# The 256th score of every query: two 16-step searches on halves of the bits against one 32-step search shared by VectorE and ScalarE

## The chip, the core and the metric

The kernel runs on one core of a Trainium2 chip. The metric is the device time of one execution in microseconds (us), taken as the median of the runs. TensorE is written PE here, its weight loads PEld, VectorE is DVE, ScalarE is ACT, GpSimd is POOL, and SP is SyncE, which issues most of the DMA transfers. The profile gives the clock that was granted to TensorE as a share of 2.4 GHz: 1.00 is 2.4 GHz and 0.50 is 1.2 GHz.

## What is computed

The program is one inference step of a two-layer decoder, for a prompt of 1024 tokens and for 8 sequences of 4 new tokens with 2048 cached positions each. The change lies in the second layer, whose attention is sparse: an indexer gives every query a score against every earlier key, the 256 best keys are kept, and attention runs over those alone.

```python
def index_scores(qi, wi, ki):
    s = jnp.einsum('bthd,bsd->bths', qi, ki).astype(jnp.float32)
    return jnp.einsum('bths,bth->bts', jax.nn.relu(s), wi.astype(jnp.float32))

# for each block of 128 prompt queries
sc = index_scores(qib, wib, ki)
sc = jnp.where((key_pos[None, :] <= tq[:, None])[None], sc, -jnp.inf)
_, sel = lax.top_k(sc, n_sel)                     # n_sel = 256
valid = sel <= tq[None, :, None]
return sparse_attend(qb, k[b_idx, sel], v[b_idx, sel], valid)
```

The sample queries do the same over their 2048 cached keys and the new ones. `top_k` takes equal scores in the order of their position. The layer, like every one, is modulated by `silu(c) @ w + b`; the product for the last sublayer is computed in the same phase as the search.

## The kernel before

The phase of the program that matters is `index_phase`. It holds the scores of the prompt in `sc`, 128 partitions (one per query of a block) by 4224 columns of f32: six blocks of queries, whose rows are 384, 512, 640, 768, 896 and 1024 keys long (`SC0` gives where each begins). The first two blocks of the prompt have no more than 256 keys and need no search. The 32 sample queries lie in `scs`, 128 by 513, each query's keys spread over four partitions.

**The search.** The kernel keeps no sorted list. It finds each query's 256th score bit by bit: a candidate threshold is formed by setting one more bit (`c.bits` holds one constant per step), the scores that are not below it are counted, and the bit stays if the count is at least 256. There are seven thresholds per partition (`NC`), one for each of the six blocks and one for the sample queries, in `fbits`. In a step (`search_step`, L1161 to L1175) DVE forms the candidate `cand` (L1163), counts the sample scores (L1165), counts the six blocks (L1182), reads from PSUM the sample count that PE has summed over the four partitions (L1168), compares the counts with 256 (L1170) and updates `fbits` (L1172). The next step needs that result, so the steps stand in a row. A count is a `tensor_scalar` that compares, with `accum_out` summing the row:

```python
dve.tensor_scalar(junk[:, w], sch[:, w], cf[:, b:b + 1], 0.0, ALU.is_ge, ALU.add, accum_out=cnt[:, b:b + 1])
```

The search runs in two halves. The first 16 steps (L1184) count on `sch`, the upper 16 bits of the scores as bf16, copied beforehand (L1159). Then L1190 to L1203 count what lies above, mark the scores whose upper half equals the found one and cut out their lower 16 bits. The second 16 steps (L1213) count on those, with one conversion and one addition more per step (L1206, L1211). L1215 puts the two halves together. After that every block is counted once more on the f32 scores, ties are settled by position with a scan, and the mask for the attention is written (L1219 to L1254).

**What runs beside it.** PE has a queue in program order: `total(i)` (L1067), the sum of the sample counts for step i, stands between the pieces of the modulation product. For each of its 12 units of weights u (`MU`), the order is total(2u), `multiply(u)` (L179), total(2u+1), `turn(u)` (L192). A multiply is 8 matmuls of 256 columns in f32, which the profile shows as 16 passes. The weights of a unit, 1 MB, land in `vT`, which holds one unit: SP issues the load of unit u+1 (L975) when multiply(u) has finished with it (`used`).

```python
for i in range(2 * MU):
    total(i)
    if i % 2 == 0:
        if i:
            pe.wait_ge(row_ready, i // 2)
        mod.multiply(pe, i // 2)
    else:
        mod.turn(pe, i // 2)
```

ACT copies the sums of a unit out of PSUM (L186) and has nothing else to do during the search. Behind the weights SP issues 16 loads of the sample cache (L1440). When DVE is through with the masks, all engines meet and the attention of the prompt begins.

Of the kernel before, what the change touches and what calls it, by code (L numbers as in the profile page):

```python
# [40 lines left out]
MU = 3 * D // 256  # L41
# [859 lines left out]
def index_phase(nc, c, d):  # L901

    with ExitStack() as ctx:
        sb = lambda n, s, dt=F32: ctx.enter_context(nc.sbuf_tensor(f"ix_{n}", s, dt))
        sem = lambda n: c.new_sem(f"ix_{n}")
        sc = sb("sc", [P, SCW])
# [10 lines left out]
        fbits, cand, acc = sb("fbits", [P, NC], I32), sb("cand", [P, NC], I32), sb("acc", [P, NC], I32)  # L917
        cnt, part, need = sb("cnt", [P, NC]), sb("part", [P, 3]), sb("need", [P, NC + 1])
        tot = sb("tot", [P, 2, 3])
        thi, above, candf, keep = sb("thi", [P, NSEL]), sb("above", [P, NSEL]), sb("candf", [P, NSEL]), sb("keep", [P, NSEL], I32)  # L920
        mrow = rs[0:NSQ, :, 0:256]
        junk = sb("junk", [P, SCW], BF16)

# [2 lines left out]

        cum = rel[:, 0:2, :]
        words = rel[:].rearrange("p a n -> p (a n)").bitcast(BF16)
        sch, junks = words[:, 0:SCW], words[:, SCW:SCW + SKW + 1]
# [177 lines left out]
        @block.vector  # L1107
        def _(dve):
            k = [0]

            def link(ins):

                k[0] += 1
                ins.then_inc(step, 1)
                dve.wait_ge(step, k[0])
# [13 lines left out]
            n = 0  # L1129
# [21 lines left out]
            link(dve.tensor_tensor(scs[:, SKW:SKW + 1], c.ps[:, 7, 0:1], c.newkey[:, 0:1], ALU.add))  # L1151


            link(dve.tensor_copy(fbits[:], c.bits[:, 0:1].to_broadcast([P, NC])))
            dve.wait_ge(causal, NSEL)
            cf, ff = cand[:].bitcast(F32), fbits[:].bitcast(F32)
# [4 lines left out]
            def search_step(i, s0, prompt_counts, extra):  # L1161

                dve.tensor_tensor(cand[:], fbits[:], c.bits[:, bass.ds(i, 1)].to_broadcast([P, NC]), ALU.bitwise_xor).then_inc(sel, 1)  # L1163
                dve.wait_ge(sel, s0 + 1)
# [9 lines left out]
                dve.wait_ge(sel, s0 + (10 + extra))
                dve.wait_ge(part_ready, i + 1)  # L1175

            def blocks():
                return [(b, slice(SC0[q], SC0[q] + (q + 1) * P)) for b, q in enumerate(BLK)]

            def upper_counts(s1):  # L1180
                for b, w in blocks():
                    dve.tensor_scalar(junk[:, w], sch[:, w], cf[:, b:b + 1], 0.0, ALU.is_ge, ALU.add, accum_out=cnt[:, b:b + 1]).then_inc(sel, 1)  # L1182

            with dve.Fori(0, 16) as i:  # L1184
                search_step(i, i * 10, upper_counts, 0)

            link(dve.tensor_copy(thi[:], fbits[:, 0:NSEL].bitcast(BF16).rearrange("p (n two) -> p n two", two=2)[:, :, 1]))  # L1190
            for b, w in blocks():
                ins = dve.tensor_scalar(junk[:, w], sch[:, w], thi[:, b:b + 1], 0.0, ALU.is_gt, ALU.add, accum_out=above[:, b:b + 1])
            link(ins)
            for b, w in blocks():
                ins = dve.tensor_scalar(junk[:, w].bitcast(I16), sch[:, w], thi[:, b:b + 1], -1.0, ALU.is_equal, ALU.mult)
            link(ins)
            low = sc[:].bitcast(U16).rearrange("p (n two) -> p n two", two=2)[:, :, 0]
            for b, w in blocks():
                y = junk[:, w].bitcast(U16)
                ins = dve.scalar_tensor_tensor(out=y, in0=low[:, w], scalar=fbits[:, b:b + 1].bitcast(U16)[:, 0:1], in1=y,  # L1200
                                               op0=ALU.bitwise_xor, op1=ALU.bitwise_and)
            link(dve.tensor_copy(keep[:], fbits[:, 0:NSEL]))
            link(dve.tensor_tensor(fbits[:, 0:NSEL], keep[:], keep[:], ALU.bitwise_xor))  # L1203

            def lower_counts(s1):
                dve.tensor_copy(candf[:], cand[:, 0:NSEL]).then_inc(sel, 1)  # L1206
                dve.wait_ge(sel, s1 + 1)
                for b, w in blocks():
                    dve.tensor_scalar(sch[:, w], junk[:, w].bitcast(U16), candf[:, b:b + 1], 0.0, ALU.is_ge, ALU.add, accum_out=cnt[:, b:b + 1]).then_inc(sel, 1)
                dve.wait_ge(sel, s1 + 7)  # L1210
                dve.tensor_tensor(cnt[:, 0:NSEL], cnt[:, 0:NSEL], above[:], ALU.add).then_inc(sel, 1)  # L1211
# [541 lines left out]
def build(nc, d):  # L1753
    with ExitStack() as ctx:
# [19 lines left out]
        c.bits = sb("bits", [P, 32], I32)  # L1774
# [45 lines left out]
def tables():  # L1820
# [91 lines left out]
```

## Time and profile before

| | us |
|---|---|
| median of 3 runs (lowest to highest) | 3023.41 (3021.97 to 3024.28) |
| the profiled execution: its span, first to last instruction | 3025.1 |
| of it, DVE from the first instruction of the search (L1154) to the first behind it (L201) | 1350.13 to 1597.86 |
| the first 16 steps | 112.0 |
| between the two halves | 13.6 |
| the second 16 steps | 119.2 |

The profiled execution is 1.7 us above the median of the runs. The stretches of the table are read from the table of busy times by window. In such a table a row is a stretch in us from the start of the span; behind its length stands the busy time of each engine with the number of its instructions, and then the granted clock of PE, the busy share of the DMA engines and GB/s. In the timelines a row is the start in us, the duration in us, the engine, the line, the operation, what it writes and reads, and in brackets how long the engine was idle before it and whom it waited for. In the groups, the two numbers behind the bar are busy time in us and the mean duration of one instruction in ns. Instructions of one engine overlap a little: the distance between two starts is shorter than the duration of the first.

### The profile page before, as it was taken

To read this page: it belongs to the slowest core of one execution; us is meant where nothing else is said; L and a number is where in the kernel's file an instruction comes from. 1 tells how busy PE (TensorE), PEld (TensorE's weight loads), DVE (VectorE), ACT (ScalarE), POOL (GpSimd) and SP (SyncE) were. 2 spreads that over 40 slices of the span, in tenths; PEclk is the share of its full clock that TensorE was granted. 3 is DMA by queue.
4 is the path that set the end of the run, shared out by engine and by line. 5 is a ranking of instruction groups with operands and counts; after the bars stand their busy time and mean duration, and the time that the engine had idled before them with its cause. 6 is when DMAs were issued, how large, how long until landed. Compare 5 with 4: busy or idle time off the path is not lost. (4 is left out here: it accounts for less than half of the span.)

```text
span 3025.1 us, 40642 instructions
## 1 busy us (share of the span) xinstructions
PE 2520.1 (83%) x14573; PEld 2225.2 (74%) x14573; DVE 1439.8 (48%) x3100; ACT 694.4 (23%) x1162; POOL 744.9 (25%) x557
## 2 busy tenths in 40 slices
PE   7866999999999689784312789697869999999995
PEld 3446999999999589741112567345869999999994
DVE  2747333333333730179997578344273333333336
ACT  2113111111110322150001888312131111111101
POOL 0223121121121235410000677521131211221110
PEclk9887999999999799896655999888979999999997
DMA  9421111111110234552121110571011111111101
GB/s 368 166 94 56 42 42 42 42 42 69 42 42 14 99 113 162 152 121 81 56 69 28 39 32 16 182 268 56 29 56 42 42 42 42 42 64 47 42 14 57
DMA packets 89864, 230.67 MB, mean 76 GB/s; under 512 B 15764, under 2 KB 52724, under 8 KB 73396
## 3 DMA queue, kind: packets, MB, share of 16 engines
q1 hardware_dynamic: 75856, 205.33, 19.6%
q0 software_dynamic: 10400, 22.18, 2.3%
q10 hardware_dynamic: 3524, 2.07, 0.2%
q8 instruction: 49, 0.80, 0.1%
q14 instruction: 35, 0.29, 0.0%
HBM read 200.77 MB, written 28.76 MB: 76 GB/s over the span
## 5 line engine op out<-in xcount | busy, mean ns | idle before, releaser
L676 PE MATMUL ps<-f_hhi,f_whi 128*128 128x352 f32 x2112 | 687.2, 325 | 33.9 <-DVE f_hlo L348 18.4
L677 PE MATMUL ps<-f_hhi,f_wlo 128*128 128x352 f32 x2112 | 681.7, 323 | 0.0
L678 PE MATMUL ps<-f_hlo,f_whi 128*128 128x352 f32 x2112 | 680.9, 322 | 0.0
L647 POOL TENSOR_TENSOR f_wlo<-f_raw,f_whi 128x2048 fp32r<-128x2048 f32 x66 | 304.0, 4607 | 1110.1 <-ACT f_whi L623 1110.1
L80 DVE SCALAR_TENSOR_TENSOR xT<-ps,mod,xT 128x352 f32<-128x352 f32 (+1 forms) x576 | 327.9, 572 | 219.8 <-PE ps L698 121.4
L676 PEld LDWEIGHTS ps<-f_hhi,f_whi 128*128 128x128 f32 x2112 | 400.4, 190 | 37.6 <-DVE f_hlo L348 37.6
L677 PEld LDWEIGHTS ps<-f_hhi,f_wlo 128*128 128x128 f32 x2112 | 401.0, 190 | 0.0
L678 PEld LDWEIGHTS ps<-f_hlo,f_whi 128*128 128x128 f32 x2112 | 400.1, 189 | 0.0
L696 PE MATMUL ps<-f_ahi,f_whi 128*128 128x352 f32 x1056 | 340.6, 323 | 0.0
L697 PE MATMUL ps<-f_ahi,f_wlo 128*128 128x352 f32 x1056 | 338.3, 320 | 0.0
L698 PE MATMUL ps<-f_alo,f_whi 128*128 128x352 f32 x1056 | 338.1, 320 | 0.0
L623 ACT ACTIVATE f_whi<-f_raw 128x2048 fp32r<-128x2048 f32 x66 | 126.4, 1915 | 554.2 <-PE ps L698 418.2
L1396 POOL TENSOR_TENSOR pa_pr<-pa_pr,pa_rl 128x128 f32<-128x128 f32 (+7 forms) x128 | 142.8, 1147 | 368.1 <-DVE pa_rl L1376 368.0
L716 DVE TENSOR_TENSOR f1n_g<-f1n_sq,ps 128x352 f32<-128x352 f32 x66 | 34.4, 521 | 399.4 <-PE ps L678 396.9
L716 DVE TENSOR_TENSOR f0n_g<-f0n_sq,ps 128x352 f32<-128x352 f32 x66 | 34.4, 521 | 398.1 <-PE ps L678 395.7
L697 PEld LDWEIGHTS ps<-f_ahi,f_wlo 128*128 128x128 f32 x1056 | 198.4, 188 | 0.0
L696 PEld LDWEIGHTS ps<-f_ahi,f_whi 128*128 128x128 f32 x1056 | 198.1, 188 | 0.0
L698 PEld LDWEIGHTS ps<-f_alo,f_whi 128*128 128x128 f32 x1056 | 197.9, 187 | 0.0
L876 PE MATMUL ps<-pj_hhi,pj_whi 128*128 128x352 f32 x408 | 135.0, 331 | 19.0 <-DVE pj_hlo L354 11.0
L1067 PE MATMUL ps<-ix_part,rowsum 128*128 128x1 f32 x64 | 16.3, 324 | 156.3 <-DVE ix_rel L1165 156.2
L179 PE MATMUL ps<-ada_raw,silu 128*9 128x256 f32 x576 | 129.2, 388 | 14.5 <-ACT silu L431 14.5
L1316 PE MATMUL ps<-kst,pa_qst 128*128 128x512 f32 (+3 forms) x192 | 75.2, 392 | 73.7 <-DMA pa_qst<-halves 41.7
(307 smaller groups left out, 3939.0 us busy)
## 6 DMA issues: line engine op xcount, KB each, us to landing
f_raw<-in_ffn SPq DMA_DIRECT2D x66, 1024.0 KB, 4.8
ada_raw<-in_ada SPq DMA_DIRECT2D x36, 1024.0 KB, 5.0
sa_kv<-in_ckv POOLq DMA_DIRECT2D x54, 256.0 KB, 4.3
ix_vT<-in_ada SPq DMA_DIRECT2D x12, 1024.0 KB, 4.8
sa_kv<-in_ckv SPq DMA_DIRECT2D x42, 256.0 KB, 4.4
pj_raw<-in_win SPq DMA_DIRECT2D x9, 1024.0 KB, 5.8
pa_qst<-halves SPq DMA_DIRECT2D x128, 64.0 KB, 2.4
halves<-pj_shi SPq DMA_DIRECT2D x45, 176.0 KB, 1.9
```

The costliest lines, as they stand in the source:

```text
L80: ins = dve.scalar_tensor_tensor(out=x, in0=psum[:, 0:n], scalar=gate[:, 0:1], in1=x, op0=ALU.mult, op1=ALU.add)
L179: last = pe.matmul(self.sums(u), self.c.silu[:, k, :], w[:, k, :], start=(k == 0), stop=(k == KD - 1))
L623: act.activation(whi[:, a, :], raw[:, a % 2, :], ACT.Copy).then_inc(w_hi, 1)
L647: pool.tensor_tensor(wlo[:, a, :], raw[:, a % 2, :], whi[:, a, :].bitcast(F32), ALU.subtract).then_inc(w_lo, 1)
L676: pe.matmul(c.ps[:, bank, 0:CH], hi[:, k, side, :], hhi[:, k, col], start=(k == 0), stop=False)
L677: pe.matmul(c.ps[:, bank, 0:CH], lo[:, k, side, :], hhi[:, k, col], start=False, stop=False)
L678: last = pe.matmul(c.ps[:, bank, 0:CH], hi[:, k, side, :], hlo[:, k, col], start=False, stop=(k == KD - 1))
L696: pe.matmul(c.ps[:, q % 6, 0:CH], hi[:, k, w], ahi[:, k, col], start=(k == 0), stop=False)
L697: pe.matmul(c.ps[:, q % 6, 0:CH], lo[:, k, w], ahi[:, k, col], start=False, stop=False)
L698: last = pe.matmul(c.ps[:, q % 6, 0:CH], hi[:, k, w], alo[:, k, col], start=False, stop=(k == 1))
L876: pe.matmul(c.ps[:, q, 0:CH], hi[:, k, w], hhi[:, k, col], start=(k == 0), stop=False)
L1396: pool.tensor_tensor(p, p, rl[:, i % 3, g:g + 1].to_broadcast([P, (q + 1) * P]), ALU.mult).then_inc(p_ready, 1)
```

## The change

The two halves become one loop of 32 steps that counts on the f32 scores themselves. There is no upper half, no lower half and nothing between them. In each step DVE counts the sample scores and the three short blocks (384, 512 and 640 keys); ACT counts the three long blocks (768, 896 and 1024) with `Sign`: the sum of the signs of (candidate − score) over a row tells how many scores lie below. `signs(i)` waits for the candidate of step i (`cand_ready`), and DVE waits for the three sums (`signs_ready`) before it compares all counts with the limits in `lim`. The candidate for the next step is formed in one operation with the update of the last. A score that equals the candidate gives a sign of 0, so a threshold of the long blocks can end a step beside a tied score; this is settled once at the end (L1202 to L1214). PE's queue and SP's keep their order.

```diff
+            def signs(i):
+                act.wait_ge(cand_ready, i + 1)
+                for b, w in blocks(SGN):
+                    last = act.activation(junk[:, w], sc[:, w], ACT.Sign, bias=cand[:, b:b + 1].bitcast(F32), scale=-1.0,
+                                          accum_out=cnt[:, b:b + 1])
+                last.then_inc(signs_ready, 1)
+
             for u in range(MU):
+                signs(2 * u)
+                signs(2 * u + 1)
                 mod.copy_sums(act, u)
+            with act.Fori(2 * MU, 32) as i:
+                signs(i)
...
-            link(dve.tensor_copy(sch, sc[:].bitcast(BF16).rearrange("p (n two) -> p n two", two=2)[:, :, 1]))
...
+            with dve.Fori(0, 32) as i:
+                s0 = i * (SGN + 3)
                 dve.tensor_scalar(junks[:], scs[:], cf[:, NSEL:NC], 0.0, ALU.is_ge, ALU.add, accum_out=part[:, 0:1]).then_inc(part_ready, 1)
-                prompt_counts(s0 + 1)
+                for b, w in blocks(0, SGN):
+                    dve.tensor_scalar(junk[:, w], sc[:, w], cf[:, b:b + 1], 0.0, ALU.is_lt, ALU.add, accum_out=cnt[:, b:b + 1]).then_inc(sel, 1)
                 dve.wait_ge(tot_ready, i + 1)
+                dve.tensor_scalar(diff[:, NSEL:NC], c.ps[:, 4, 0:1], TOPK - 0.5, None, ALU.subtract).then_inc(sel, 1)
+                dve.wait_ge(signs_ready, i + 1)
+                dve.wait_ge(sel, s0 + SGN)
+                dve.tensor_tensor(diff[:, 0:NSEL], lim[:], cnt[:, 0:NSEL], ALU.subtract).then_inc(sel, 1)
...
+                dve.tensor_scalar(miss[:], diff[:].bitcast(I32), 31, c.bits[:, bass.ds(i, 1)], ALU.arith_shift_right, ALU.bitwise_and).then_inc(sel, 1)
...
+                dve.scalar_tensor_tensor(out=cand[:], in0=cand[:], scalar=c.bits[:, bass.ds(i + 1, 1)], in1=miss[:],
+                                         op0=ALU.bitwise_xor, op1=ALU.bitwise_xor).then_inc(cand_ready, 1)
+                dve.wait_ge(cand_ready, i + 2)
...
+            for b, w in blocks(SGN):
+                y = cum[:, b % 2, 0:w.stop - w.start]
+                dve.tensor_scalar(junk[:, w], sc[:, w], cf[:, b:b + 1], 0.0, ALU.is_gt, ALU.add, accum_out=cnt[:, b:b + 1])
+                link(dve.tensor_scalar(y, sc[:, w], cf[:, b:b + 1], -1.1 * NEG, ALU.is_le, ALU.mult))
+                link(dve.tensor_tensor_reduce(out=y, in0=y, in1=sc[:, w], scale=1.0, scalar=-NEG, op0=ALU.add, op1=ALU.min, accum_out=above[:, b:b + 1]))
```

On ACT, before, the copies of the modulation sums stand alone during the search, behind the last ReLU of the scores (`ix_rs` is the row buffer of the sums):

```order
L1103 ACTIVATE ix_rn<-ps 128x4
L186 ACTIVATE ix_rs<-ps 9x256 x12
```

and now six counts, those of two steps, stand ahead of each copy:

```order
L1115 ACTIVATE ix_junk,ix_cnt<-ix_sc,ix_cand 128x896
L1115 ACTIVATE ix_junk,ix_cnt<-ix_sc,ix_cand 128x1024
L186 ACTIVATE ix_rs<-ps 9x256
L1115 ACTIVATE ix_junk,ix_cnt<-ix_sc,ix_cand 128x768
L1115 ACTIVATE ix_junk,ix_cnt<-ix_sc,ix_cand 128x896
L1115 ACTIVATE ix_junk,ix_cnt<-ix_sc,ix_cand 128x1024
```

The copies kept their order among themselves; 96 counts moved onto the engine around them.

On DVE a step of the first loop was, before, from the candidate to the update (REGISTER_ALU rows work out the number that a wait compares with):

```order
L1163 TENSOR_TENSOR ix_cand<-ix_fbits,bits 128x7
L1164 ISA
L1165 TENSOR_SCALAR ix_rel,ix_part<-ix_rel,ix_cand 128x513
L1182 TENSOR_SCALAR ix_junk,ix_cnt<-ix_rel,ix_cand 128x384
L1182 TENSOR_SCALAR ix_junk,ix_cnt<-ix_rel,ix_cand 128x512
L1182 TENSOR_SCALAR ix_junk,ix_cnt<-ix_rel,ix_cand 128x640
L1182 TENSOR_SCALAR ix_junk,ix_cnt<-ix_rel,ix_cand 128x768
L1182 TENSOR_SCALAR ix_junk,ix_cnt<-ix_rel,ix_cand 128x896
L1182 TENSOR_SCALAR ix_junk,ix_cnt<-ix_rel,ix_cand 128x1024
L1167 REGISTER_ALU
L1168 TENSOR_SCALAR ix_acc<-ps 128x1
```

and now the step is, with three counts fewer and one wait more (the ISA row of L1189 waits for ACT):

```order
L1183 TENSOR_SCALAR ix_rel,ix_part<-ix_rel,ix_cand 128x513
L1185 TENSOR_SCALAR ix_junk,ix_cnt<-ix_sc,ix_cand 128x384
L1185 TENSOR_SCALAR ix_junk,ix_cnt<-ix_sc,ix_cand 128x512
L1185 TENSOR_SCALAR ix_junk,ix_cnt<-ix_sc,ix_cand 128x640
L1186 REGISTER_ALU
L1187 TENSOR_SCALAR ix_diff<-ps 128x1
L1189 ISA
L1190 TENSOR_TENSOR ix_diff<-ix_lim,ix_cnt 128x6
```

The sums of the sample scores still come first, and the read of PE's total still stands behind the counts.

PE's rows of this stretch are the same in both kernels; a unit of the modulation with the totals around it reads, in the changed kernel:

```order
L1073 MATMUL ps<-ix_part,rowsum 128x1
L179 MATMUL ps<-ix_vT,silu 9x256 x8
L1073 MATMUL ps<-ix_part,rowsum 128x1
L192 MATMUL ps<-ident,ix_rs 128x9 x2
L1073 MATMUL ps<-ix_part,rowsum 128x1
```

So the total of every odd step stands behind a multiply, as it did before.

## Rows read from the trace of the kernel before

**Rows 1.** The profile's first line.

```profile
span 3025.1 us, 40642 instructions
```

**Rows 2.** Busy times by window: first half, between, second half of the search.

```profile
1352.90:1464.90 112.00, 54.92 (x176) 22.62 (x176) 104.88 (x288) 2.99 (x8) 0.00 (x0) 0.69 0.21 75
1464.90:1478.50 13.60, 0.00 (x0) 0.00 (x0) 12.94 (x27) 0.00 (x0) 0.00 (x0) 0.50 0.00 1
1478.50:1597.70 119.20, 31.57 (x104) 15.19 (x104) 110.58 (x321) 1.49 (x4) 0.00 (x0) 0.60 0.19 62
```

**Rows 3.** DVE's timeline: the search's first row, its second step, the first row behind.

```profile
1350.13 0.17 DVE L1154 COPY ix_fbits<-bits 128x7 int32<-128x7 int32 x1
...
1360.17 0.75 DVE L1165 TENSOR_SCALAR_CACHE_REDUCE ix_rel<-ix_rel,ix_cand 128x513 bf16<-128x513 f32 x1
...
1360.84 0.61 DVE L1182 TENSOR_SCALAR_CACHE_REDUCE ix_junk<-ix_rel,ix_cand 128x384 bf16<-128x384 bf16 x1
...
1362.84 1.00 DVE L1182 TENSOR_SCALAR_CACHE_REDUCE ix_junk<-ix_rel,ix_cand 128x768 bf16<-128x768 bf16 x1
...
1366.04 0.15 DVE L1168 TENSOR_SCALAR ix_acc<-ps 128x1 int32<-128x1 f32 x1
1366.15 0.17 DVE L1170 TENSOR_SCALAR ix_acc<-ix_cnt 128x6 int32<-128x6 f32 x1
1366.36 0.23 DVE L1172 SCALAR_TENSOR_TENSOR ix_fbits<-ix_acc,bits,ix_fbits 128x7 int32<-128x7 int32 x1
1366.98 0.17 DVE L1163 TENSOR_TENSOR ix_cand<-ix_fbits,bits 128x7 int32<-128x7 int32 x1 [0.39 <-DVE ix_fbits L1172]
...
1597.86 0.38 DVE L201 TENSOR_TENSOR mod<-ps,vec 128x216 f32<-128x216 f32 x1
```

**Rows 4.** DVE's groups of 1024 columns: counts, a comparison, sums of two tensors.

```profile
L1182 DVE TENSOR_SCALAR_CACHE_REDUCE ix_junk<-ix_rel,ix_cand 128x1024 bf16<-128x1024 bf16 x16 | 20.4, 1275 | 0.0
L1363 DVE CUSTOM_DVE_ANT_0 pa_pr<-ps,mb 128x1024 f32<-128x1024 f32 x16 | 19.4, 1215 | 0.0
L1140 DVE SCALAR_TENSOR_TENSOR ix_sc<-ix_rel,wtok,ix_sc 128x1024 f32<-128x1024 f32 x7 | 9.0, 1284 | 0.8 <-ACT ix_rel L1093 0.2
L1248 DVE SCALAR_TENSOR_TENSOR ix_vT<-ix_rel,ix_need,ix_vT 128x1024 bf16<-128x1024 f32 x1 | 1.3, 1285 | 0.0
L1244 DVE TENSOR_SCALAR_CACHE_REDUCE ix_junk<-ix_sc,ix_fbits 128x1024 bf16<-128x1024 f32 x1 | 1.3, 1279 | 0.0
L1245 DVE TENSOR_SCALAR ix_vT<-ix_sc,ix_fbits 128x1024 bf16<-128x1024 f32 x1 | 0.8, 750 | 0.0
```

**Rows 5.** ACT's groups: the exponentials of the prompt's attention, which sum their rows.

```profile
L1425 ACT ACTIVATION_READ_ACCUMULATOR pa_pr<-pa_pr,pa_nb 128x1 f32 x128 | 24.2, 189 | 0.0
L1425 ACT ACTIVATE pa_pr<-pa_pr,pa_nb 128x1024 f32<-128x1024 f32 x16 | 18.4, 1148 | 0.2
L1425 ACT ACTIVATE pa_pr<-pa_pr,pa_nb 128x896 f32<-128x896 f32 x16 | 16.7, 1042 | 0.3
L1425 ACT ACTIVATE pa_pr<-pa_pr,pa_nb 128x768 f32<-128x768 f32 x16 | 15.0, 934 | 0.4
```

**Rows 6.** The loads of the modulation weights: issues, and time to landing.

```profile
L975 SPq DMA_DIRECT2D ix_vT<-in_ada x12: 328/328/592, 1331.8 to 1515.6; - x12
...
DMA to landing us min/median/max: 4.8/4.8/22.3
```

**Rows 7.** PE: the multiplies as a group, one burst, one total; then warm weight loads.

```profile
L179 PE MATMUL ps<-ix_vT,silu 128*9 128x256 f32 x192 | 68.3, 534 | 0.0
...
1368.51 6.41 PE L179 MATMUL ps<-ix_vT,silu 128*9 128x256 f32 x16
...
1375.01 0.38 PE L1067 MATMUL ps<-ix_part,rowsum 128*128 128x1 f32 x2
...
1357.27 1.60 PEld L179 LDWEIGHTS ps<-ix_vT,silu 128*9 128x9 f32 x8 [0.15 <-issue]
```

**Rows 8.** Busy times by window: inside a multiply, right after another, and later.

```profile
1368.60:1374.30 5.70, 5.70 (x14) 1.81 (x15) 5.24 (x15) 0.00 (x0) 0.00 (x0) 0.51 0.00 0
1430.30:1435.50 5.20, 0.60 (x4) 0.49 (x4) 5.20 (x13) 0.37 (x1) 0.00 (x0) 1.00 0.54 202
1435.70:1438.60 2.90, 0.47 (x2) 0.47 (x2) 2.44 (x11) 0.00 (x0) 0.00 (x0) 0.50 0.00 0
```

More of the change, by code:

```diff
@@ L916, in index_phase @@
         NC = NSEL + 1
-        fbits, cand, acc = sb("fbits", [P, NC], I32), sb("cand", [P, NC], I32), sb("acc", [P, NC], I32)
+        cand, miss = sb("cand", [P, NC], I32), sb("miss", [P, NC], I32)
+        lim, diff = sb("lim", [P, NSEL]), sb("diff", [P, NC])
         cnt, part, need = sb("cnt", [P, NC]), sb("part", [P, 3]), sb("need", [P, NC + 1])
         tot = sb("tot", [P, 2, 3])
-        thi, above, candf, keep = sb("thi", [P, NSEL]), sb("above", [P, NSEL]), sb("candf", [P, NSEL]), sb("keep", [P, NSEL], I32)
+        tie, above = sb("tie", [P, 2, NSEL]), sb("above", [P, NSEL])
         mrow = rs[0:NSQ, :, 0:256]
@@ L928, in index_phase @@
         words = rel[:].rearrange("p a n -> p (a n)").bitcast(BF16)
-        sch, junks = words[:, 0:SCW], words[:, SCW:SCW + SKW + 1]
+        junks = words[:, SCW:SCW + SKW + 1]
         eq = vT[:, 0, :].bitcast(BF16)[:, 0:2 * SEQ].rearrange("p (a n) -> p a n", a=2)
@@ L937, in index_phase @@
         step, sel, tot_ready, ws_ready = sem("step"), sem("sel"), sem("tot_ready"), sem("ws_ready")
+        cand_ready, signs_ready = sem("cand_ready"), sem("signs_ready")
         part_ready, ki_out, ada_ready = sem("part_ready"), sem("ki_out"), sem("ada_ready")
@@ L941, in index_phase, with blocks @@
         BLK = list(range(SEL0, QT))
+        SGN = 3
+        def blocks(first=0, last=NSEL):
+            return [(b, slice(SC0[BLK[b]], SC0[BLK[b]] + (BLK[b] + 1) * P)) for b in range(first, last)]
         mod = Modulation(c, mrow, lambda u: vT[:].rearrange("p a n -> p (a n)")[:, 0:UNIT], lambda pe, u: pe.wait_ge(ada_ready, 16 * (u + 1)),
@@ L1151, in _ @@
             link(dve.tensor_tensor(scs[:, SKW:SKW + 1], c.ps[:, 7, 0:1], c.newkey[:, 0:1], ALU.add))
-            link(dve.tensor_copy(fbits[:], c.bits[:, 0:1].to_broadcast([P, NC])))
+            for b, w in blocks():
+                dve.memset(lim[:, b:b + 1], float(w.stop - w.start - TOPK) + (0.5 if b < SGN else TOPK - 510.5))
             dve.wait_ge(causal, NSEL)
-            cf, ff = cand[:].bitcast(F32), fbits[:].bitcast(F32)
-            link(dve.tensor_copy(sch, sc[:].bitcast(BF16).rearrange("p (n two) -> p n two", two=2)[:, :, 1]))
@@ L1174, in search_step @@
[L1174 to L1185, printed above, removed]
@@ L1190, in _ @@
[L1190 to L1196, printed above, removed]
@@ L1197, in _ @@
[L1197 to L1211, printed above, removed]
@@ L1213, in _ @@
-            with dve.Fori(16, 32) as i:
-                search_step(i, i * 12 - 32, lower_counts, 2)
-            link(dve.tensor_tensor(fbits[:, 0:NSEL], fbits[:, 0:NSEL], keep[:], ALU.bitwise_xor))
+                dve.tensor_scalar(diff[:, NSEL:NC], c.ps[:, 4, 0:1], TOPK - 0.5, None, ALU.subtract).then_inc(sel, 1)
+                dve.wait_ge(signs_ready, i + 1)
+                dve.wait_ge(sel, s0 + SGN)
+                dve.tensor_tensor(diff[:, 0:NSEL], lim[:], cnt[:, 0:NSEL], ALU.subtract).then_inc(sel, 1)
@@ new lines, in _ @@
+                dve.wait_ge(sel, s0 + (SGN + 2))
+                dve.tensor_scalar(miss[:], diff[:].bitcast(I32), 31, c.bits[:, bass.ds(i, 1)], ALU.arith_shift_right, ALU.bitwise_and).then_inc(sel, 1)
+                dve.wait_ge(sel, s0 + (SGN + 3))
+                dve.scalar_tensor_tensor(out=cand[:], in0=cand[:], scalar=c.bits[:, bass.ds(i + 1, 1)], in1=miss[:],
+                                         op0=ALU.bitwise_xor, op1=ALU.bitwise_xor).then_inc(cand_ready, 1)
+                dve.wait_ge(cand_ready, i + 2)
@@ new lines, in _ @@
+            ff = cf
+            sg = slice(SGN, NSEL)
+            link(dve.tensor_scalar(tie[:, 1, sg], cf[:, sg], 2.0 ** -126, None, ALU.is_ge))
+            link(dve.scalar_tensor_tensor(out=tie[:, 0, sg], in0=cf[:, sg], scalar=-2.0 ** -126, in1=tie[:, 1, sg], op0=ALU.is_le, op1=ALU.max))
+            link(dve.tensor_tensor(cf[:, sg], cf[:, sg], tie[:, 0, sg], ALU.mult))
+            for b, w in blocks(SGN):
[3 more added lines that the diff above has]
+                link(dve.tensor_tensor_reduce(out=y, in0=y, in1=sc[:, w], scale=1.0, scalar=-NEG, op0=ALU.add, op1=ALU.min, accum_out=above[:, b:b + 1]))
@@ L1217, in _ @@
+            link(dve.tensor_scalar(tie[:, 0, sg], cnt[:, sg], TOPK - 0.5, None, ALU.is_ge))
+            dve.tensor_tensor(above[:, sg], above[:, sg], tie[:, 0, sg], ALU.mult)
+            link(dve.tensor_scalar(tie[:, 1, sg], tie[:, 0, sg], 1.0, -NEG, ALU.subtract, ALU.mult))
+            link(dve.tensor_tensor(above[:, sg], above[:, sg], tie[:, 1, sg], ALU.add))
+            link(dve.tensor_tensor(cf[:, sg], cf[:, sg], above[:, sg], ALU.max))
             mod.apply(dve, SUBS - 1, MU, 0, link)
@@ L1773, in build @@
         c.invc = sb("invc", [P, 4, 16])
-        c.bits = sb("bits", [P, 32], I32)
+        c.bits = sb("bits", [P, 33], I32)
         c.rowsum, c.before = sb("rowsum", [P, P]), sb("before", [P, P])
@@ L1829, in tables @@
     t["invc"] = inv
-    bits = [-1] + [1 << (30 - i) for i in range(31)]
+    bits = [-1] + [1 << (30 - i) for i in range(31)] + [0]
     t["bits"] = np.tile(np.array(bits, np.int32), (P, 1))
```

12 lines of the change are left out of this document (3 added, 9 removed).

## The prediction

> **What bounds the kernel now.** The span is 3025.1 us [rows 1], 1.7 us above the median of the runs, so a saving in the profile is taken off the median as it stands. I read first the busy times by window of the search [rows 2]: DVE works in 104.88 of 112.00 us of the first half, 12.94 of 13.60 us between the halves and 110.58 of 119.20 us of the second, while ACT works for 4.5 us in all and PE for 86. DVE's timeline [rows 3] then shows why: a step is one string of instructions, the only gap is 0.39 us at the turn of the loop, and each step needs the result of the last. From the first row to the first behind the search it is 1597.86 − 1350.13 = 247.7 us. All engines meet behind it, so a us less here is a us less in the end.
>
> **What a step costs now and then.** Before, it is 112.00/16 = 7.0 us and 119.20/16 = 7.45 us [rows 2]. Its parts [rows 3]: sample count 0.67 (1360.17 to 1360.84), three short blocks 2.00 (to 1362.84), three long blocks 3.20 (to 1366.04), then the comparisons and update.
>
> The change counts on f32 instead of 16-bit words. That costs DVE nothing: the 1024-column count takes 1275 ns on bf16 and 1279 ns on f32 [rows 4]. So DVE's work ahead of its waits is the turn of the loop, 0.40, and 0.67 + 2.00 + 0.08 for the last sum: 3.15 us after the candidate. The first comparison (0.12 to the next start) ends at 3.27.
>
> ACT's part has no row of its own. The nearest is the exponential, which also takes a bias per partition and sums its row: 934, 1042 and 1148 ns for the three lengths, and 189 ns to read a sum [rows 5]. Back to back the read hides behind the next instruction except the last: 0.93 + 1.04 + 1.15 − 0.10 + 0.19 = 3.21 us. With 0.05 us of signalling at each end it is 3.3 us after the candidate. From below it is bounded by DVE's own 3.27, since ACT's rows all rise by 0.84 ns a column and none is faster; from above I keep 3.8, half a us for signalling and for a sign slower than the exponential. The two engines end level, at 3.3. Then come three small operations in a row; by the distances of L1170 and L1172 (0.21) and the 0.23 of the last [rows 3], 0.65. **A step by itself is 3.3 + 0.65 + 0.1 of slack for the new waits = 4.05 us**, range 3.9 to 4.6. Queued behind DVE's new wait for ACT are only these three operations; behind ACT's wait for the candidate stands one copy of sums for every six counts, 2.99/8 = 0.37 us [rows 2], which fits into the 0.65 us when ACT has nothing to do.
>
> **Where 4.05 us does not decide.** PE's queue keeps its order, and that is the term I weigh most. The total of an odd step stands behind a multiply. The multiplies form a chain of their own: a burst ends, SP issues the next MB, it lands 4.8 us later [rows 6], the next burst runs. A burst takes 68.3/12 = 5.69 us on average and 6.41 in the row shown [rows 7]. Two steps before took 14 us, which hid 4.9 (with 0.1 for signalling) + 5.69 = 10.6 us entirely; two steps of 4.05 take 8.1 us and do not. So in the first 24 steps a pair of steps costs one load and one burst.
>
> What a burst takes depends on the clock. Inside the 6.41 us burst the granted clock is 0.51, 1.2 GHz, for its first 14 passes, 0.41 us apiece; at 2.4 GHz eight weight loads stand in 1.60 us, 0.20 apiece [rows 7, 8]. The clock goes up during a burst and has come down before the next: after one burst it was still 1.00 in 1430.3 to 1435.5, and 0.50 from 1435.7 [rows 8]. Bursts now follow one another after 4.9 us instead of 14.0 − 5.69 = 8.3, so some will begin before the clock has fallen. I take 5.3 us, somewhat under the mean of 5.69, and **10.2 us for a pair**. Bounds: sixteen passes at 0.20 give 3.3, a pair of 8.2, which is no longer than two steps; sixteen at 0.41 give 6.6, a pair of 11.5.
>
> The Trainium skill ("TensorE: Matmul & The Clock Gate", section "HAM oscillation — how this bites in real kernels") says that a burst of matmuls shorter than the DMA wait after it starts at the low clock every time. By that rule no burst would begin at 2.4 GHz, and the pair would be the rows' mean or more. The trace agrees in part: it shows the low clock at the start of a burst (0.51), but after gaps of 8.3 us.
>
> **The sum.** The first weights are issued at 1331.8 and land after 22.3 us, at 1354.1 [rows 6]; DVE is ready earlier (the bf16 copy ahead of the loop falls away, seven small fills come instead), so multiply 0 starts at 1354.1 in any case and hides the setup. Eleven pairs: 112.2. The last burst: 5.3. Its total, the comparisons and the update, 0.4 + 0.05 + 0.12 + 0.65 = 1.2. Step 24 starts at 1354.1 + 112.2 + 5.3 + 1.2 = 1472.8. Eight steps alone: 32.4, to 1505.2.
>
> Then the ties, new: per long block a count, a comparison and a reduction of two tensors; at 1024 columns 1279 + 750 + 1215 ns [rows 4], the last from the nearest row, which reads PSUM. The three blocks are 2688 columns, 2.625 times that, 8.5 us; nine small operations at some 0.2 us and the reads of sums bring it to **11 us**, range 9.5 to 13. The search ends at 1516.2 in place of 1597.86: **81.7 us less**. The rest of the span, mask, attention and the second FFN, is untouched; the 16 cache loads move ahead with the end of the weights and have the last steps and the masks to land. Forecast: 3025.1 − 81.7 = 2943.4 us in the profile, **2942 us** as a median.
>
> **The rivals.** *Cold bursts*: every burst runs at 1.2 GHz throughout, 6.6 us, because PE's gaps let the clock fall each time. Eleven pairs longer by 1.3 and one burst: 11 × 1.3 + 1.3 = 16 us more, 2958. For it speaks the burst of 6.41; against it that the mean is 5.69. *Warm bursts*: the shorter gap keeps 2.4 GHz. A pair then costs 8.2, 11 × 2.0 + 2.0 = 24 us less, 2918; two steps of 4.05 set the same floor. The clock's 5.2 us of grace [rows 8] speaks for it, the 0.51 inside the burst of 1368.60 against it. *No overlap*: ACT and DVE both read `sc`, and would slow each other until a step is the sum of both parts, 3.15 + 3.3 + 0.65 = 7.1 us: 32 × 7.1 + 11 = 238 of the 247.7 us, 10 less, 3014; the change would then not do what it says. Against it: the DVE sum of 1024 columns takes 1284 ns with ACT writing beside it and 1285 ns with ACT idle [rows 4]. *Slow signs*, the one that ends slower than before: if a sign summed on ACT takes over twice the exponential's time, the counts last 6.7 us, a step 7.4, and 32 × 7.4 + 11 = 248 us is what the search takes today; at two and a half times, 8.0 us, a step is 8.7 and the search 289 us, 42 more, so 3066. The trace shows ACT at 1148 ns against DVE's 1275 for 1024 columns, so this needs an effect that no row has.
>
> The Trainium skill ("ScalarE: Activation LUTs", section "Rules for kernel authors") advises VectorE over ScalarE for simple elementwise work, up to about three times faster per element in bf16; that speaks against this change. With its factor of three the signs would last 3 × 3.2 = 9.6 us, a step 10.4 and the kernel, as an estimate, 3120. The trace disagrees for counts: on DVE they gain nothing from bf16 (1275 against 1279 ns), and ACT's rows are the shorter ones.
>
> **How the numbers follow.** Forecast 0.68 (with its own bounds, pairs of 9.7 to 10.8, steps and ties: 2933 to 2953), cold bursts 0.14, warm bursts 0.14, no overlap 0.02, slow signs 0.02. The range must take in the forecast and one side beside it: from 2930, part of the way to warm bursts, to 2960, which holds cold bursts: 0.68 + 0.14 and a little. Faster by over 0.2% (6 us, about what a measurement of this kernel can tell from no change): 0.97; slower 0.02; within 0.01.
>
> **What would show it.** In the profile after, the groups of signs should read about 0.93, 1.04 and 1.15 us; the first 24 steps should start in pairs some 10.2 us apart, with DVE idle in every odd step behind PE's total and not behind ACT; the last eight steps should stand 4.05 us apart with both engines done within 0.2 us; the clock should be near 0.5 at the start of most bursts. Wrong would be pairs of 8.2 us with DVE waiting for ACT (the loads do not bind), signs longer than the exponentials, or a search that shrank while the span did not.

## The result, and the profile after

| | before | after |
|---|---|---|
| median (lowest to highest) | 3023.85 us (3021.97 to 3029.91), 4 runs | 2943.67 us (2942.05 to 2944.72), 4 runs |
| ratio, 95% interval | | 0.9727 [0.9714, 0.9739] |
| profiled span | 3025.1 | 2942.1 |
| from the first sample count to the first instruction behind the search | 1353.13 to 1597.86 | 1349.28 to 1516.46 |
| from there to the end of the span | 1427.2 | 1425.6 |

The forecast was 2942.0, the range 2930 to 2960. The gain lies in the search: it ends 81.4 us earlier, and behind it the kernel takes what it took, but for 1.6 us. Of the 81.4 us, 1.2 had come about before the search: DVE's copy of the sample scores ahead of it (L1150, now L1169) starts at 1348.11 us in after and at 1349.35 in before, and that is scatter, for in the changed kernel once more (e8, below) it starts at 1350.02. Lines have moved by a few; L1183 is now the sample count (L1165), L1185 a DVE count (L1182), L1115 a sign on ACT, L1190, L1192 and L1194 the comparison and the update, L1073 the total (L1067), L981 the load (L975). Where [rows 1] stood, the page of after has:

```profile
span 2942.1 us, 40633 instructions
```

The window of the first 24 steps answers to [rows 2] (same columns: length, busy PE, PEld, DVE, ACT, POOL, clock, DMA share, GB/s):

```profile
1348.90:1472.40 123.50, 74.60 (x264) 30.30 (x264) 83.27 (x295) 81.21 (x157) 0.00 (x0) 0.83 0.32 111
```

DVE was busy 94% of the first half of the old search; in the first 24 steps it is now busy 83.27 of 123.50 us, 67%, and ACT 81.21. No engine is full in this window, so the time must lie in a chain that passes from engine to engine. The waits of the search (who waited for whom: total us, times, longest) name it:

```profile
PE ps L179 <- DMA ix_vT<-in_ada: 25.3, 12, 2.3
DVE ix_diff L1187 <- PE ps L1073: 22.6, 12, 2.1
DVE ix_rel L1183 <- DVE ix_cand L1194: 11.8, 31, 0.4
DVE ix_diff L1190 <- ACT ix_junk L1115: 0.3, 1, 0.3
```

DVE waits 12 times for PE's total, about 1.9 us each, in the odd steps only, and PE waits 12 times for weights. PE's timeline shows the period (its rows answer to [rows 7]):

```profile
1352.52 5.31 PE L179 MATMUL ps<-ix_vT,silu 128*9 128x256 f32 x16 [2.05 <-DMA ix_vT<-in_ada]
1357.76 0.38 PE L1073 MATMUL ps<-ix_part,rowsum 128*128 128x1 f32 x2
...
1362.81 5.30 PE L179 MATMUL ps<-ix_vT,silu 128*9 128x256 f32 x16 [2.05 <-DMA ix_vT<-in_ada]
...
1465.51 5.21 PE L179 MATMUL ps<-ix_vT,silu 128*9 128x256 f32 x16 [2.13 <-DMA ix_vT<-in_ada]
```

The total of the odd step stands right behind the burst. From the first burst to the twelfth it is 1465.51 − 1352.52 = 113.0 us, 10.27 a pair of steps: a burst of 5.2 us and 5.0 us from its end to the start of the next. The loads still land in 4.8 us as in [rows 6]; the longest, 22.1 us, is the first:

```profile
L981 SPq DMA_DIRECT2D ix_vT<-in_ada x12: 327/328/592, 1330.4 to 1460.5; - x12
...
DMA to landing us min/median/max: 4.8/4.8/22.1
```

The same wait from DVE's side, in its timeline; then the last candidate and the first row behind the search:

```profile
1349.28 0.75 DVE L1183 TENSOR_SCALAR_CACHE_REDUCE ix_rel<-ix_rel,ix_cand 128x513 bf16<-128x513 f32 x1 [0.23 <-DVE ix_cand L1176]
...
1358.17 0.16 DVE L1187 TENSOR_SCALAR ix_diff<-ps 128x1 f32<-128x1 f32 x1 [1.72 <-PE ps L1073]
1358.28 0.17 DVE L1190 TENSOR_TENSOR ix_diff<-ix_lim,ix_cnt 128x6 f32<-128x6 f32 x1
...
1505.74 0.23 DVE L1194 SCALAR_TENSOR_TENSOR ix_cand<-ix_cand,bits,ix_miss 128x7 int32<-128x7 int32 x1
...
1516.46 0.38 DVE L201 TENSOR_TENSOR mod<-ps,vec 128x216 f32<-128x216 f32 x1
```

The last eight steps have no burst in them and stand 4.24 us apart. One of them, in the timeline of all engines, from a candidate to the next:

```profile
1476.08 0.23 DVE L1194 SCALAR_TENSOR_TENSOR ix_cand<-ix_cand,bits,ix_miss 128x7 int32<-128x7 int32 x1
1476.34 0.93 ACT L1115 ACTIVATE ix_junk<-ix_sc,ix_cand 128x768 bf16<-128x768 f32 x1 [1.05 <-DVE ix_cand L1194]
1476.68 0.75 DVE L1183 TENSOR_SCALAR_CACHE_REDUCE ix_rel<-ix_rel,ix_cand 128x513 bf16<-128x513 f32 x1 [0.38 <-DVE ix_cand L1194]
...
1479.33 0.18 ACT L1115 ACTIVATION_READ_ACCUMULATOR ix_junk<-ix_sc,ix_cand 128x1 f32 x1
...
1479.35 0.15 DVE L1187 TENSOR_SCALAR ix_diff<-ps 128x1 f32<-128x1 f32 x1
1479.65 0.17 DVE L1190 TENSOR_TENSOR ix_diff<-ix_lim,ix_cnt 128x6 f32<-128x6 f32 x1
1479.95 0.23 DVE L1192 TENSOR_SCALAR ix_miss<-ix_diff,bits 128x7 int32<-128x7 int32 x1
1480.31 0.23 DVE L1194 SCALAR_TENSOR_TENSOR ix_cand<-ix_cand,bits,ix_miss 128x7 int32<-128x7 int32 x1
```

Both engines are through at 1479.5, within 0.1 us of each other. ACT is the later one by a little. Its path adds up to the step: 0.26 to its first sign, 3.17 to the end of its last sum, 0.14 to the comparison, then 0.30 and 0.36 to the next candidate, 4.23 in all. DVE's own path does not: 0.60 to the sample count, 2.67 to L1187, 0.11 to the comparison (the distance at 1358.17, where ACT had long been done; it is 0.11 in the last steps of e3 too, where ACT has less to do), 0.30 and 0.36 give 4.04. So ACT sets the step, by 0.19 us.

The groups of signs, which answer to the exponentials of [rows 5] (busy us, mean ns):

```profile
L1115 ACT ACTIVATE ix_junk<-ix_sc,ix_cand 128x1024 bf16<-128x1024 f32 x32 | 36.2, 1133 | 0.0
L1115 ACT ACTIVATE ix_junk<-ix_sc,ix_cand 128x896 bf16<-128x896 f32 x32 | 32.8, 1026 | 0.0
L1115 ACT ACTIVATE ix_junk<-ix_sc,ix_cand 128x768 bf16<-128x768 f32 x32 | 29.9, 935 | 33.5 <-DVE ix_cand L1194 31.7 <-DVE ix_cand L1176 1.8
L1115 ACT ACTIVATION_READ_ACCUMULATOR ix_junk<-ix_sc,ix_cand 128x1 f32 x96 | 17.9, 186 | 0.0
```

A sign takes what an exponential takes, with DVE reading the same scores beside it. DVE is not slowed either: its counts of 384 keys take 608 ns on average here, in before and in e4, where ACT counts nothing. The clock inside one burst (start 1404.1), by window, answers to [rows 8]:

```profile
1404.10:1404.50 0.40, 0.40 (x2) 0.11 (x3) 0.27 (x2) 0.00 (x0) 0.00 (x0) 0.50 0.00 0
1404.60:1407.50 2.90, 2.90 (x9) 0.93 (x8) 2.52 (x8) 2.86 (x5) 0.00 (x0) 0.53 0.02 6
1407.90:1409.20 1.30, 1.30 (x7) 0.39 (x5) 0.00 (x0) 0.00 (x0) 0.00 (x0) 1.00 0.00 0
1413.00:1414.00 1.00, 0.00 (x0) 0.00 (x0) 0.86 (x4) 0.86 (x2) 0.00 (x0) 1.00 0.40 164
```

The burst starts at 1.2 GHz and ends at 2.4. The clock then stays at 2.4 GHz to within 0.3 us of the next burst (start 1414.28), although PE does nothing in 1413.0 to 1414.0, and that burst reads 0.50 again in its first 0.4 us. Of the twelve bursts ten read 0.50 in their first 0.4 us, the other two 0.72 and 0.64. The Trainium skill ("TensorE: Matmul & The Clock Gate", section "HAM oscillation — how this bites in real kernels") describes a kernel whose bursts are shorter than the wait for their data, and start at the low clock every time. The trace agrees with it on ten of twelve starts, though a burst here, at 5.2 us, is not shorter than the 5.0 us between two of them.

### The profile page after: what moved, and what is told of

Read it like the earlier page. It is cut to its first block and busy times, and to the rows that moved or that the text cites. A ratio compares the mean times of both kernels' runs of the same rounds, so it can differ in the third digit from the quotient of the medians.

```text
span 2942.1 us, 40633 instructions
## 1 busy us (share of the span) xinstructions
PE 2510.8 (85%) x14573; PEld 2220.6 (75%) x14573; DVE 1328.1 (45%) x2876; ACT 796.7 (27%) x1354; POOL 743.8 (25%) x557
## 5 line engine op out<-in xcount | busy, mean ns | idle before, releaser
L877 PE MATMUL ps<-pj_hhi,pj_wlo 128*128 128x352 f32 x408 | 133.8, 328 | 0.0
```

What stands on the lines that cost most here:

```text
L877: pe.matmul(c.ps[:, q, 0:CH], lo[:, k, w], hhi[:, k, col], start=False, stop=False)
```

## The experiments

Three theories stood. *Loads and bursts*: in the first 24 steps a pair of steps costs one load and one burst, whatever a step costs; the last eight cost a step each. *The step*: what DVE and ACT do in a step, and the small operations behind it, sets the time throughout. *Contention*: one engine slows the other. Every edit below is made on the changed kernel. The median of before on these chips was 3027.24 us for the first four (12 runs) and 3025.77 for the last four (7 runs). Beside the median I give the search, from the first sample count to L201, 167.2 us in after, since the rest of the span scatters: from 1416.9 (e6) and 1418.6 (e3) to 1427.7 us (e4), with nothing changed in it. A difference in the medians of less than 10 us is therefore read from the search.

**e1: a second buffer for the weights.** Units land by turns in `vT` and in `rel`, which is idle during the search, so a load no longer waits for the burst before it.

```diff
+        wbuf = [t[:].rearrange("p a n -> p (a n)")[:, 0:UNIT] for t in (vT, rel)]
...
-                if u:
-                    sp.wait_ge(mod.used, u)
+                if u > 1:
+                    sp.wait_ge(mod.used, u - 1)
+                elif u:
+                    sp.wait_ge(r_used, NIH * NSEL)
...
-                sp.dma_start(vT[:].rearrange("p a n -> p (a n)")[:, 0:UNIT], d.ada[(SUBS - 1) * MU + u]).then_inc(ada_ready, 16)
+                sp.dma_start(wbuf[u % 2], d.ada[(SUBS - 1) * MU + u]).then_inc(ada_ready[u % 2], 16)
```

> The changed kernel with a second buffer for the modulation weights (in the score buffer that the search no longer uses), so that unit u+1 is loaded while unit u is multiplied. Theory (in the first 24 steps a pair of steps is bound by one load of 4.8 us and one burst of 5.2 us in a row, 10.27 us): without the load in the row a pair is two steps of 4.24 us, 8.5 us; 11 pairs shorter by 1.8 and no wait of 2 us for the first weights: some 20 to 22 us less than the changed kernel's 2943.7, so 2922 to 2924. Rival (the pairs are bound by ACT's counts and the waits between the engines): pairs stay at 10.27, 2942 to 2945.

Measured: 2927.83 us (2927.49 to 2929.66), ratio to before 0.9675 [0.9659, 0.9691]; search 148.4 us, 18.8 less. PE's timeline and one of the waits of e1 (its lines are three further down):

```profile
1362.66 3.62 PE L179 MATMUL ps<-ix_rel,silu 128*9 128x256 f32 x16
...
1371.33 5.49 PE L179 MATMUL ps<-ix_vT,silu 128*9 128x256 f32 x16
...
1379.68 3.62 PE L179 MATMUL ps<-ix_rel,silu 128*9 128x256 f32 x16
```

```profile
DVE ix_diff L1190 <- PE ps L1076: 3.1, 6, 2.1
```

No burst waits for weights any more (the first apart, which waits 2.4 us), a pair takes some 8.5 us, twice 4.24, and DVE's waits for the total shrink from 22.6 us to 3.1. The search gained a little less than the 20 to 22 us expected; the expectation had left out that wait for the first weights. So the loads were what bound the pairs, and the next floor, two steps, lies 1.8 us under them. The bursts now alternate: 3.62 us with the clock at 1.00 throughout (1362.70 to 1366.20), then 5.49 us with 0.50 at its start (1371.40 to 1373.00); why they do was not tried, and the steps wait for neither.

**e2: PE's gaps filled.** Matmuls of 128 columns into an unused part of PSUM, whose results nothing reads, keep PE occupied while it would wait: eight ahead of a burst and six behind each turn.

```diff
+            def filler(n):
+                for _ in range(n):
+                    pe.matmul(c.ps[:, 0, 0:P], c.rowsum[:, :], c.before[:, :], start=True, stop=True)
...
+                        filler(8)
                         pe.wait_ge(row_ready, i // 2)
                     mod.multiply(pe, i // 2)
                 else:
                     mod.turn(pe, i // 2)
+                    if i + 1 < 2 * MU:
+                        filler(6)
```

> The changed kernel with matmuls of 128 columns into an unused PSUM bank in PE's idle time between the bursts (8 ahead of a burst, 6 behind a turn; their results are not used). Theory (a burst takes 5.2 us because it runs mostly at 1.2 GHz): the granted clock stays at 1.00, a burst takes 3.4 us, a pair 4.9 + 3.4 = 8.3 or two steps of 4.24 = 8.5, so 2922 to 2925. Rival (the fillers delay the totals, or the clock falls all the same): pairs of 10.3 to 11, 2943 to 2952.

Measured: 2923.3 us (2920.18 to 2930.13), ratio 0.9661 [0.9642, 0.968]; search 150.2 us. PE's timeline of e2, and two windows of PE alone, the burst and the stretch behind it:

```profile
1373.68 3.61 PE L179 MATMUL ps<-ix_vT,silu 128*9 128x256 f32 x16 [0.79 <-DMA ix_vT<-in_ada]
...
1382.25 3.61 PE L179 MATMUL ps<-ix_vT,silu 128*9 128x256 f32 x16
```

```profile
1373.70:1377.20 3.50, 3.50 (x16) 1.00 0.03 7
1377.30:1382.20 4.90, 4.40 (x34) 1.00 0.62 214
```

With work in the gaps the clock stays at 1.00 from the second burst on, the burst takes 3.61 us instead of 5.2 and the pair 8.7 on average instead of 10.27. This is the rival of the warm bursts, made to happen: it had been priced at 2918, with 3.3 us for a burst and 4.05 for a step.

**e3: two blocks on ACT in place of three.** DVE counts the block of 768 keys too.

```diff
-        SGN = 3
+        SGN = 4
```

> The changed kernel with four blocks counted on DVE (384 to 768) and two on ACT. A step by itself becomes 4.24 + 0.94 - 0.2 = 5.0 us. Theory (load and burst bind the first 24 steps): the pairs stay at 10.3, since two steps of 5.0 fit; only the last 8 steps grow by 0.75 us each, 6 us, and the ties shrink by one block, 2.6 us: 2945 to 2949. Rival (steps decide everywhere): 32 x 0.75 - 2.6 = 21 us more, 2965.

Measured: 2943.98 us (2940.1 to 2949.46), ratio 0.9731 [0.9713, 0.9749]; search 171.1 us, 3.9 more. A step by itself rose from 4.24 to 4.98, and the first 24 steps took 123.4 us, against 123.2 in after. PE's timeline of e3:

```profile
1384.35 5.23 PE L179 MATMUL ps<-ix_vT,silu 128*9 128x256 f32 x16 [2.17 <-DMA ix_vT<-in_ada]
...
1394.58 5.24 PE L179 MATMUL ps<-ix_vT,silu 128*9 128x256 f32 x16 [2.09 <-DMA ix_vT<-in_ada]
```

Three quarters of a us more in every step left the first 24 where they were: only the last eight paid, 5.9 us, of which the ties gave some 2.3 back, with one long block fewer. That speaks against the theory of the step for those 24. The 4.98 also bears out the sum of DVE's path: 4.04 and the 0.93 by which a count of 768 keys moves the next (below, in e4's rows) give 4.97.

**e4: no signs at all.** DVE counts all six blocks on f32, in one loop of 32 steps; ties need no settling then.

```diff
-        SGN = 3
+        SGN = 6
...
-                signs(2 * u)
-                signs(2 * u + 1)
                 mod.copy_sums(act, u)
...
-                dve.wait_ge(signs_ready, i + 1)
```

> The changed kernel with all six blocks counted on DVE and none on ACT, and without the settling of ties, which nothing needs then: the 32 steps on f32 scores alone. A step is 4.24 + 0.94 + 1.07 + 1.20 - 0.2 = 7.25 us, two of them 14.5 us hide load and burst. Theory (the gain comes from ACT's share; the f32 steps alone save only what stood between the halves): 32 x 7.25 + 0.4 = 232.4 us of search against 247.7 before, so 3024 - 15 = 3008 to 3012. Rival (f32 counts or the shorter string of small operations carry a gain of their own): below 2990.

Measured: 3020.47 us (3011.77 to 3022.66; 9 runs), ratio 0.9973 [0.9963, 0.9983]; search 240.5 us, steps of 7.52. DVE's timeline of e4:

```profile
1503.41 1.01 DVE L1173 TENSOR_SCALAR_CACHE_REDUCE ix_junk<-ix_sc,ix_cand 128x768 bf16<-128x768 f32 x1
...
1504.34 1.14 DVE L1173 TENSOR_SCALAR_CACHE_REDUCE ix_junk<-ix_sc,ix_cand 128x896 bf16<-128x896 f32 x1
...
1506.73 0.17 DVE L1177 TENSOR_TENSOR ix_diff<-ix_lim,ix_cnt 128x6 f32<-128x6 f32 x1
1507.03 0.23 DVE L1179 TENSOR_SCALAR ix_miss<-ix_diff,bits 128x7 int32<-128x7 int32 x1
1507.51 0.22 DVE L1181 SCALAR_TENSOR_TENSOR ix_cand<-ix_cand,bits,ix_miss 128x7 int32<-128x7 int32 x1 [0.25 <-DVE ix_miss L1179]
1508.25 0.75 DVE L1171 TENSOR_SCALAR_CACHE_REDUCE ix_rel<-ix_rel,ix_cand 128x513 bf16<-128x513 f32 x1 [0.52 <-DVE ix_cand L1181]
```

The search ends at 1590.61, 7.3 us before that of [rows 3]: that is what f32 and one loop are worth by themselves, and the rest of the gain comes from ACT's share. The median lies above the 3008 to 3012 expected. The counts are as long as on bf16 ([rows 3]: 1.00 us for 768 keys). The step was expected 0.27 us shorter. The difference sits in two distances, L1179 to L1181 (0.48; 0.36 in after) and from there to the next count (0.74; 0.60); why they are longer here was not tried.

**e5: each load twice.** From the second unit on, SP issues a second load of the same MB into `rel`, whose content nothing uses, and the burst waits for both.

```diff
...
+                if u:
+                    if u == 1:
+                        sp.wait_ge(r_used, NIH * NSEL)
+                    sp.dma_start(rel[:].rearrange("p a n -> p (a n)")[:, 0:UNIT], d.ada[(SUBS - 1) * MU + u]).then_inc(more_ready, 16)
```

> The changed kernel with every load of modulation weights from the second on followed by a second load of the same 1 MB into a scratch buffer, and PE waiting for both before its burst. Theory (load and burst in a row bind the first 24 steps): a pair grows by the time of 1 MB, some 2.6 us at the 400 GB/s that a load reaches, and by up to 1 us for bursts that begin colder: 11 x (2.6 to 3.6) = 29 to 40 us more than the changed kernel on the same chip. Rival (the search waits for ACT or for the small operations): 0 to 5 us more.

Measured: 2984.4 us (2982.74 to 2984.69), ratio 0.9863 [0.9846, 0.9879]; search 203.9 us, 36.7 more. PE's timeline and the waits of e5:

```profile
1366.24 5.94 PE L179 MATMUL ps<-ix_vT,silu 128*9 128x256 f32 x16 [4.39 <-DMA ix_rel<-in_ada]
...
1379.77 6.00 PE L179 MATMUL ps<-ix_vT,silu 128*9 128x256 f32 x16 [4.46 <-DMA ix_rel<-in_ada]
```

```profile
DVE ix_diff L1191 <- PE ps L1077: 59.3, 12, 5.4
PE ps L179 <- DMA ix_rel<-in_ada: 49.0, 11, 4.7
```

From the second burst on the pairs take 13.6 us, 3.4 more: 2.4 by PE's longer wait for the load (about 4.45 against 2.1), 0.8 by a burst that runs longer at the low clock (0.50 in the whole of 1366.30 to 1370.30) behind a longer gap, and 0.2 by the total ahead of that wait (0.59 us against 0.38). Even steps stay at 4.24 us and odd ones take the whole price, 9.4. That is the chain, lengthened at one link.

**e6: the 32 steps written out.** DVE's loop becomes 32 copies of its body; waits compare with constants, the step's column of `bits` is named by a constant, and there is no turn of a loop.

```diff
-            with dve.Fori(0, 32) as i:
+            for i in range(32):
...
-                dve.tensor_scalar(miss[:], diff[:].bitcast(I32), 31, c.bits[:, bass.ds(i, 1)], ALU.arith_shift_right, ALU.bitwise_and).then_inc(sel, 1)
+                dve.tensor_scalar(miss[:], diff[:].bitcast(I32), 31, c.bits[:, i:i + 1], ALU.arith_shift_right, ALU.bitwise_and).then_inc(sel, 1)
...
```

> The changed kernel with DVE's 32 steps written out, so that no wait compares with a number worked out in a register and no branch stands between two steps. Theory (a step by itself is 4.24 us and not the forecast 4.05 because the small operations stand 0.30 and 0.36 us apart, and the next count 0.60 behind the last, for the sake of registers and the branch; the pairs hang on PE): the last 8 steps shrink to some 3.7 us, the pairs stay at 10.27: 4 to 5 us less than the changed kernel. Rival (the gaps are the engine's own latency): 0. Rival (steps bind everywhere): 16 us less.

Measured: 2938.34 us (2933.1 to 2941.49), ratio 0.9714 [0.9697, 0.973]; search 164.9 us, 2.3 less. A step by itself takes 3.95 us, the pairs stay at 10.3. DVE's timeline of e6, from a comparison to the next step:

```profile
1499.51 0.17 DVE L1190 TENSOR_TENSOR ix_diff<-ix_lim,ix_cnt 128x6 f32<-128x6 f32 x1 [0.39 <-ACT ix_junk L1115]
1499.71 0.23 DVE L1192 TENSOR_SCALAR ix_miss<-ix_diff,bits 128x7 int32<-128x7 int32 x1
1499.98 0.23 DVE L1194 SCALAR_TENSOR_TENSOR ix_cand<-ix_cand,bits,ix_miss 128x7 int32<-128x7 int32 x1
1500.24 0.75 DVE L1183 TENSOR_SCALAR_CACHE_REDUCE ix_rel<-ix_rel,ix_cand 128x513 bf16<-128x513 f32 x1
```

The small operations stand 0.20 and 0.27 us apart, where after had 0.30 and 0.36, and the next count follows after 0.26 instead of 0.60. Yet the step lost only 0.29 of the 0.5 that was expected: DVE now waits 0.39 us for ACT in each step, and ACT's string of signs is the floor.

**e7: e6 and e1 together.**

> The steps written out and a second buffer for the weights. Theory: with the load out of the row the step binds everywhere, so writing it out is worth 32 x 0.5 us here against 8 x 0.5 without the buffer: a pair of some 7.4 us unless a cold burst of over 5.5 us holds the total of the odd step; 16 + 12 to 16 us less than the changed kernel. Rival (PE's cold bursts become the bound): pairs stay near 8.3, 16 to 19 us less.

Measured: 2917.57 us (2911.99 to 2918.83), ratio to before 0.9643 [0.9627, 0.9659]; search 140.0 us. Nearly all steps are 3.95 us apart, whether a burst lies in them or not. Without the loads in the way, what e6 saves in a step counts in nearly every step: 140.0 against 148.4 in e1. Against e8 the search is 27.5 us shorter, just short of the 28 to 32 expected, since a step did not reach 3.7 us. It is the fastest of the kernels here.

**e8: the changed kernel once more**, on the chip of the last four.

> The changed kernel itself once more, on the same chip as the three above, to compare them with. 0.972 to 0.974 of the kernel before.

Measured: 2944.92 us (2942.61 to 2947.22), ratio 0.973 [0.9714, 0.9747]; search 167.5 us, pairs and steps as in after.

## Why the prediction was right, point by point

| | forecast | measured |
|---|---|---|
| first multiply starts | 1354.1 | 1352.5 |
| eleven pairs | 112.2 | 113.0 |
| from the last burst's start to step 24 | 6.5 | 6.6 |
| eight steps | 32.4 | 33.9 |
| ties | 11 | 10.5 |
| the search ends | 1516.2 | 1516.5 |

As in the forecast, a step begins at the end of a candidate: step 24 at 1472.07 and the ties at 1505.97.

**Counting on f32 costs DVE nothing**: held. The counts last as long (e4's rows), and the move to f32 and one loop by itself is worth some 7 us (e4).

**A sign costs what an exponential costs**: held: 935, 1026 and 1133 ns against 934, 1042 and 1148. The rival of the slow signs falls with it, and so does the estimate of 3120 that was worked out from the Trainium skill ("ScalarE: Activation LUTs", section "Rules for kernel authors", VectorE rather than ScalarE for simple work). The trace disagrees: for counts that sum their rows DVE is the slower engine here, bf16 or not (1275 and 1279 ns for 1024 columns, against 1133 on ACT).

**The engines overlap**: held. *No overlap* had said steps of 7.1 us; with both engines on the scores DVE's counts (608 ns for 384 keys, with ACT counting or not) and ACT's signs keep their lengths.

**A pair costs one load and one burst**: held, 10.27 us against 10.2, with DVE behind PE's total and not behind ACT, as the last paragraph of the prediction asked. Both terms held: 5.0 us from a burst's end to the next against 4.9, and 5.2 for the burst against 5.3. e1 took the load out of the chain and the pair fell to two steps; e5 lengthened the load and the pair rose; e2 shortened the burst and it fell; e3 and e6 changed the step by +0.74 and −0.29 us and it did not move. Of that set only the theory of loads and bursts has all five signs right.

**The burst between the two rivals**: the choice of 5.3 us was right by its size (5.2), and less so by its reason, so that it came this close is in part luck. I had expected some bursts to begin before the clock fell; hardly any did. They begin at 1.2 GHz, and are shorter than the 5.69 us of before because the clock rises sooner inside them: 3.2 us into the burst at 1404.10, where in before it took 4.2 to 5.7 us (the bursts at 1368.51, 1410.59 and 1424.62). What sets that moment was not tried. *Cold bursts* had the start right and the rest wrong. *Warm bursts* came about where PE was kept at work (e2), and in every second burst of e1. Their price was too low, even so: a burst at 2.4 GHz takes 3.61 us and not the 3.3 that the prediction took from weight loads.

**The step by itself**: mis-sized, 4.05 forecast and 4.24 measured. The term that failed is the 0.65 for the three small operations with 0.1 of slack for the waits: it is 0.30 + 0.36 + 0.23 = 0.89 us. ACT's part ahead of it was nearly right, 0.03 + 3.17 + 0.14 = 3.34 from the end of one candidate to the comparison against 3.3; the 0.05 us of signalling at each end, which stood in no row, measured 0.03 and 0.14. The 0.21 that I had taken from [rows 3] is the distance of two operations with a wait between them too, L1170 and L1172, but there DVE's queue works out one register number (L1171), and in the changed kernel two, the second in the line that takes the step's column of `bits` (first the changed kernel, then the row of before; duration in ns min/median/max):

```profile
L1191 DVEq ALU_OP  x32: 40/40/40, 1352.4 to 1505.1; - x32
...
L1192 DVEq FUSED_REGOPS  x32: 46/46/46, 1352.6 to 1505.3; - x32
...
L1171 DVEq ALU_OP  x32: 40/40/40, 1359.1 to 1597.0; - x32
```

The same pair, L1193 and L1194, stands ahead of the next candidate. With constants in place of both (e6) the three operations take 0.20 + 0.27 + 0.23 = 0.70 us; which of the two rows costs what was not tried apart. In the eight last steps the step cost 1.5 us, and the pairs 0.8. The ties, 0.5 us under the estimate, and a start of the first multiply 1.6 us earlier than forecast (its load was issued at 1330.4, not 1331.8) gave it back. That the search ended within 0.3 us of the forecast is luck to that extent: in e8, the same kernel, the first multiply starts at 1354.3, as forecast, and the search ends at 1518.7.

## What to carry to other kernels

When an engine is relieved, look for the chain that its slowness had covered: here two steps of 7 us hid a load and a burst of 10 us, two of 4.24 did not, and a second buffer for 1 MB of weights then took 18.8 us more out of the search. Whether the clock takes part is read from windows at the start and the end of a burst, not from its mean. And the last tenths of a step in a serial loop lie between its small operations: price them by rows that have the same register work between them.

## What the hardware showed that was not expected

- Small operations in a row stand further apart in a loop, even where the data are there. From comparison to `miss` and from `miss` to `cand` it is 0.30 and 0.36 us in the loop, where two register numbers are worked out ahead of each (40 and 46 ns), and 0.20 and 0.27 us written out with constants; from `cand` to the next count 0.60 against 0.26, the turn of the loop included. e6 took out the wait numbers, the column and the turn at once, so their shares are not shown.
- The last two of these distances grew to 0.48 and 0.74 us in e4, whose loop has one wait fewer and the same register rows. What they depend on stays open.
- A burst of 16 passes took 3.61 us with PE kept at work before it, 5.2 behind a wait of about 2 us, and 6.0 behind one of 4.4 us (e5).
- Behind the search the same instructions took 1416.9 to 1427.7 us from one profile to the next. In the stretch from about 1870 to 2050 us the clock was 0.90 in after and in e8, and 0.95 in e6 and e3; why was not tried.
